# Attention stage of a two-layer diffusion step: adaLN weights in the ring, latent group first

## The reference, cut to what matters

```python
def ada_params(cvec, w, b):
    m = jax.nn.silu(cvec) @ w + b
    return jnp.split(m, N_ADA, axis=-1)

def modulate(x, g, shift, scale):
    return rms_norm(x, g) * (1.0 + scale[:, None, :]) + shift[:, None, :]

# layer 1, context tokens (group 0): 16 query heads on 4 key heads of 64, softmax with a sink logit
q, k, v = qkv_heads(h, wqkv, qn, kn)          # per-head RMS norm of q and k
s = einsum('bqkgd,bskd->bkgqs', qg, k) * HEAD_DIM ** -0.5
o = softmax([s, s_sink]) @ v;  y = o @ wo
# latent tokens (group 1): the same, q and k rotated (rope2d), keys = 128 own and 128 cached context keys
# then x = x + gate * y, and the MoE sub-layer with the last three of the six adaLN rows
```

## Time and profile before

| what | before |
|---|---|
| median of the runs | 1518.48 us (1517.93 to 1519.35) |
| the profiled execution, its own time | 1518.69 us |
| its span | 1516.9 us, so 1.8 us lie around it |
| mean granted TensorE clock | 0.948 of full |
| TensorE busy | 1429.9 us (94%) |
| VectorE, ScalarE busy | 461.3 us, 294.4 us |
| 16 DMA engines moved | 499.45 MB, 329 GB/s over the span |

### The profile page before, as it was taken

How to read it: one execution, slowest core, us unless ns; L and a number is a source line. 1 busy time by engine, 2 the same in 40 slices (tenths; PEclk the granted TensorE clock), 3 DMA queues, 4 the chain that set the end, 5 groups by cost and what they waited for, 6 DMA issues and landing times.

```text
span 1516.9 us, 23827 instructions
## 1 busy us (share of the span) xinstructions
PE 1429.9 (94%) x9544; PEld 851.1 (56%) x9544; DVE 461.3 (30%) x1449; ACT 294.4 (19%) x602; POOL 0.2 (0%) x4
## 2 busy tenths in 40 slices
PE   5798889999999999999888989999999999999997
PEld 2675775565555655556443647855565555555554
DVE  0699261222222222222234322522222222222222
ACT  2301241111111111111122212211111111111111
POOL 0000000000000000000000000000000000000000
PEclk8899889999999999999998569899999999999999
DMA  8989467699999999999744542796999999999990
GB/s 310 374 332 351 162 250 313 245 385 399 403 391 412 386 403 399 409 386 409 291 173 177 218 167 71 292 386 238 410 385 404 402 395 412 393 395 395 410 399 39
DMA packets 80640, 499.45 MB, mean 329 GB/s; under 512 B 10633, under 2 KB 15409, under 8 KB 23760
## 3 DMA queue, kind: packets, MB, share of 16 engines
q1 hardware_dynamic: 80592, 498.79, 82.2%
HBM read 497.45 MB, written 1.31 MB: 329 GB/s over the span
## 4 chain that ended last, share of the span: by engine, by line
PE 91%; DVE 5%; DMA 3%; ACT 1%; issue 1%; SPq 0%; DVEq 0%; ACTq 0%
PE ps L766 31%; PE ps L797 16%; PE ps L747 12%; PE ps L807 9%; PE ps L507 4%; PE ps L550 3%; PE ps L578 3%; PE ps L703 2%; PE ps L482 2%; PE ps L642 1%; PE ps L496 1%; PE ps L616 1%; DMA ring<-in_conv_w_dram 1%; DVE W L1188 1%; DVE hbf L1188 1%; PE ps L688 1%
## 5 line engine op out<-in xcount | busy, mean ns | idle before, releaser
L766 PE MATMUL ps<-ring,W 128*64 128x512 f32 x2048 | 453.3, 595 | 1.1 <-ACT W L1048 1.0
L766 PEld LDWEIGHTS ps<-ring,W 128*64 128x64 f32 x2048 | 166.2, 137 | 282.5 <-issue 277.6
L797 PE MATMUL ps<-ring,W 128*64 128x512 f32 x1024 | 233.9, 599 | 1.0 <-DVE W L1438 1.0
L747 PEld LDWEIGHTS ps<-W,hbf 128*128 128x128 bf16 x3168 | 183.1, 98 | 56.4 <-issue 54.2
L747 PE MATMUL ps<-W,hbf 128*128 128x128 bf16 x3168 | 199.2, 220 | 3.0 <-DVE W L1416 2.2
L1444 DVE TENSOR_TENSOR ypart<-ps,ypart 128x512 fp32r<-128x512 f32 x132 | 91.3, 692 | 191.0 <-ACT ypart L1059 191.0
L807 PE MATMUL ps<-comb,ypart 128*128 128x256 f32 x1056 | 142.5, 287 | 2.8 <-DVE ypart L1444 2.8
L1433 DVE SCALAR_TENSOR_TENSOR W<-W,ps 128x256 f32<-128x256 f32 x66 | 31.7, 480 | 352.1 <-ACT W L1053 352.1
L797 PEld LDWEIGHTS ps<-ring,W 128*64 128x64 f32 x1024 | 67.8, 136 | 117.5 <-issue 109.7
L807 PEld LDWEIGHTS ps<-comb,ypart 128*128 128x128 f32 x1056 | 130.2, 189 | 6.2 <-DVE ypart L1444 4.6
L1048 ACT ACTIVATE W<-ps 128x512 f32<-128x512 f32 x132 | 78.9, 597 | 273.7 <-PE ps L747 273.7
(11 more groups left out here) (196 smaller groups left out, 894.0 us busy)
## 6 DMA issues: line engine op xcount, KB each, us to landing
ring<-in_exp_w_gate_dram SPq DMA_DIRECT2D x128, 1024.0 KB, 8.8
ring<-in_exp_w_up_dram SPq DMA_DIRECT2D x128, 1024.0 KB, 10.8
ring<-in_exp_w_down_dram SPq DMA_DIRECT2D x128, 1024.0 KB, 9.7
S<-in_ada_w_dram SPq DMA_DIRECT2D x48, 1024.0 KB, 7.8
ring<-in_conv_w_dram SPq DMA_DIRECT2D x4, 2048.0 KB, 19.0
S<-in_attn_wqkv_dram SPq DMA_DIRECT2D x1, 6144.0 KB, 25.4
ring<-in_conv_w_dram SPq DMA_DIRECT2D x1, 4096.0 KB, 20.7
S<-in_exp_w_gate_dram SPq DMA_DIRECT2D x4, 1024.0 KB, 11.1
```

The lines of the kernel that those rows point to most:

```text
L747: mm = pe.matmul(PG[:, kk * P:(kk + 1) * P], hbf[:, part, g, 4 * half + kk, :], gbf[:, g, :], start=(n == 0), stop=(n == 2 * 3 - 1))
L766: mm = pe.matmul(PGU[64 * b:64 * b + 64, :].rearrange("p (h f) -> p h f", h=2), xg[:, k, 64 * b:64 * b + 64], gate_up_of(w[b])[:, k], star ...
L797: mm = pe.matmul(bank[64 * b:64 * b + 64, :], hidT[:, j, 64 * b:64 * b + 64], down_of(w[b])[:, j, n * 512:(n + 1) * 512], start=(j == 0), ...
```

## The change

The 16 late adaLN units no longer go to `S`. Units 32 to 37 go to ring slots 0 and 1 as soon as layer 0's pair 31 has done its down products (`pe_dn` 64), units 38 to 40 to ring slot 3 after the overflow pair's (`pe_dn` 66); units 41 to 47 reuse the same places as they are multiplied. TensorE multiplies units 32 to 35 ahead of the sum of squares, 36 to 39 behind it, 40 and 41 ahead of the head loop, and 42 to 47 in i = 0 to 5. Bank e = 4 is turned after the first three qkv products. Group 1 (latent) is multiplied, normed and transposed first, and the head loop runs its four heads first (`HEADS`). `wo` is loaded after the last qkv product. Experts 0 and 1 are loaded in the head loop (after units 43 and 46), experts 2 and 3 after the projection's first bank. `asq`, `prob`, `probT`, `oT`, `otok`, `stat` and the cached keys and values lie elsewhere, so that ring slot 3 is free.

```diff
@@ -67,7 +67,8 @@
 
     if u < EARLY:
         return u % 6
-    return u - EARLY if u < EARLY + 6 else 4 + u % 2
+    v = u - EARLY
+    return 6 + (v if v < 9 else v - 9)
 
 
...
+        ada_late = ring_f[:, 0:2 * EW].rearrange("p (s n) -> p s n", s=6)
+        ada_last = ring_f[:, 3 * EW:4 * EW].rearrange("p (s n) -> p s n", s=3)
+
+        def ada_unit(u):
+
+            slot = unit_slot(u)
+            if slot < 6:
+                return ada[:, slot, :]
+            return ada_late[:, slot - 6, :] if slot < 12 else ada_last[:, slot - 12, :]
 
         def diag(j):
...
@@ -215,21 +225,27 @@
         odd = hb_f[:, 2560:2816]
 
         arow = hT[:, 0:6, :].rearrange("p k t -> p (k t)").rearrange("p (b n) -> p b n", b=3)
+        arow_late = W[:, 3840:4352]
+
+        def ada_row(e):
+
+            return arow[:, e % 3, :] if e < 4 else arow_late
         xtok = ring_f[:, 16384:16384 + 2048].rearrange("p (g n) -> p g n", g=G)
         ytok = ring_f[:, 0:2048].rearrange("p (g n) -> p g n", g=G)
 
         B0 = 2 * EW
         qkv = ring_f[:, B0:B0 + 3072].rearrange("p (g n) -> p g n", g=G)
-        asq = ring_f[:, B0 + 3072:B0 + 5632].rearrange("p (g n) -> p g n", g=G)
-        prob = ring_f[:, B0 + 3072:B0 + 5120].rearrange("p (b h s) -> p b h s", b=2, h=QG)
-        otok = ring_f[:, B0 + 6912:B0 + 8960].rearrange("p (g n) -> p g n", g=G)
-        oT = ring_f[:, B0 + 8960:B0 + 11008].rearrange("p (k t) -> p k t", k=KC)
-        vctx = ring_f[:, B0 + 11008:B0 + 11264]
-        kctx = ring_f[:, B0 + 11264:B0 + 11520]
-        stat = ring_f[:, B0 + 11520:B0 + 11776]
+        otok = ring_f[:, B0 + 3072:B0 + 5120].rearrange("p (g n) -> p g n", g=G)
+        vctx = ring_f[:, B0 + 5120:B0 + 5376]
+        kctx = ring_f[:, B0 + 5376:B0 + 5632]
+        stat = ring_f[:, B0 + 5632:B0 + 5888]
+        asq = hb_f[:, 512:3072].rearrange("p (g n) -> p g n", g=G)
+        prob = hb_f[:, 512:2560].rearrange("p (b h s) -> p b h s", b=2, h=QG)
+        oT = hT
+        HEADS = [(1, j) for j in range(NKV)] + [(0, j) for j in range(NKV)]
         qTt = W[:, 0:2048].rearrange("p (c t) -> p c t", c=KC)
         kTt = W[:, 2048:2816].rearrange("p (c t) -> p c t", c=2)
-        probT = hb_f[:, 0:1024].rearrange("p (b n) -> p b n", b=2)
+        probT = W[:, 2816:3840].rearrange("p (b n) -> p b n", b=2)
 
         def half_of(part, h):
...
@@ -394,34 +410,40 @@
                     sp.wait_ge(moe_done, 1)
                     sp.dma_start(kctx, cache_k[0, 0].rearrange("t h d -> t (h d)")).then_inc(ld_kv, 16)
                     sp.dma_start(vctx, cache_v[0, 0].rearrange("t h d -> t (h d)")).then_inc(ld_kv, 16)
-                for s in range(2):
-                    load_expert(l, s, s, "gu")
-                for s in range(2):
-                    load_expert(l, s, s, "dn")
                 if l == 0:
+                    for s in range(2):
+                        load_expert(l, s, s, "gu")
+                    for s in range(2):
+                        load_expert(l, s, s, "dn")
                     sp.wait_ge(ada_used, EARLY)
                     load_shared(0)
                     sp.wait_ge(pj_out, 4)
+                    for s in range(2, 4):
+                        load_expert(l, s, s, "gu")
+                    for s in range(2, 4):
+                        load_expert(l, s, s, "dn")
                 else:
+                    load_ada(range(EARLY + 9, N_UNITS))
                     sp.wait_ge(at_qkv, 6)
-                    load_ada(range(EARLY, EARLY + 6))
-                    sp.wait_ge(at_nrm, 1)
-                    sp.wait_ge(at_copied, 1)
+                    sp.dma_start(wo, attn_wo[0].rearrange("(k p) n -> p k n", p=P)).then_inc(ld_wo, 16)
+                    sp.wait_ge(at_nrm, 2)
                     sp.dma_start(new_k[0, 0].rearrange("t h d -> t (h d)"),
                                  qkv[:, 0, NH * HD:(NH + NKV) * HD]).then_inc(stored, 16)
                     sp.dma_start(new_v[0, 0].rearrange("t h d -> t (h d)"),
                                  qkv[:, 0, (NH + NKV) * HD:QKVW]).then_inc(stored, 16)
-                    load_ada(range(EARLY + 6, EARLY + 8))
-                    sp.wait_ge(ada_used, EARLY + 4)
-                    sp.dma_start(wo, attn_wo[0].rearrange("(k p) n -> p k n", p=P)).then_inc(ld_wo, 16)
-                    load_ada(range(EARLY + 8, N_UNITS))
+                    for s in range(2):
+
+                        sp.wait_ge(ada_used, EARLY + 12 + 3 * s)
+                        load_expert(l, s, s, "gu")
+                        load_expert(l, s, s, "dn")
+                    sp.wait_ge(pj_out, 5)
+                    sp.wait_ge(ada_used, N_UNITS)
+                    sp.wait_ge(stored, 32)
+                    for s in range(2, 4):
+                        load_expert(l, s, s, "gu")
+                        load_expert(l, s, s, "dn")
                     sp.wait_ge(pj_out, 8)
                     load_shared(1)
-                    sp.wait_ge(stored, 32)
-                for s in range(2, 4):
-                    load_expert(l, s, s, "gu")
-                for s in range(2, 4):
-                    load_expert(l, s, s, "dn")
                 load_extra(l, 1)
...
+                    sp.wait_ge(moe_done, l + 1)
                 if l == 0:
-                    sp.wait_ge(pe_dn[0], 6)
+
                     sp.dma_start(wqkv, attn_wqkv[0].rearrange("(k p) n -> p k n", p=P)).then_inc(ld_qkv, 16)
+                    sp.wait_ge(pe_dn[0], 2 * PAIRS)
+                    load_ada(range(EARLY, EARLY + 6))
+                    sp.wait_ge(pe_dn[0], 2 * PAIRS + 2)
+                    load_ada(range(EARLY + 6, EARLY + 9))
             for g, y in enumerate((y_prompt, y_sample)):
                 sp.wait_ge(y_out, 2 * (g + 1))
...
@@ -533,7 +560,10 @@
 
             for l in range(L):
                 if l == 1:
+
+                    ada_products(range(EARLY, EARLY + 4), ps[2])
                     sum_squares(4, 0)
+                    ada_products(range(EARLY + 4, EARLY + 8), ps[2])
                 if l == 0:
 
...
@@ -589,26 +619,28 @@
                             mm.then_inc(at_tr, 1)
 
                     for n in range(3):
-                        qkv_product(0, n)
-                    qkv_product(1, 0)
-                    qkv_product(1, 1)
+                        qkv_product(1, n)
+                    ada_transposes(4, ps[2])
+                    qkv_product(0, 0)
+                    qkv_product(0, 1)
 
                     pe.wait_ge(ld_kv, 32)
                     for j in range(2):
                         mm = pe.transpose(ps[6][:, j * P:(j + 1) * P], kctx[:, j * P:(j + 1) * P], ident)
                     mm.then_inc(at_tr, 1)
-                    qk_transposes(0, ps[0:3])
-                    qkv_product(1, 2)
+                    pe.wait_ge(mod_ready, 5)
+                    qkv_product(0, 2)
+                    qk_transposes(1, ps[3:6])
 
                     def at_scores(i):
-                        g, j = divmod(i, NKV)
+                        g, j = HEADS[i]
                         keys = T if g == 0 else 2 * T
                         k0 = 0 if g == 0 else T
                         o = HD * (j % 2)
                         bk = 2 * (i % 2)
                         if i in (0, NKV):
                             pe.wait_ge(at_trc, 4 if i == 0 else 7)
-                        if i == 1:
+                        if i == 0:
                             pe.wait_ge(at_copied, 2)
                         if i >= 2:
                             pe.wait_ge(at_exp, i - 1)
...
                         mm.then_inc(at_s, 1)
 
                     def at_transposes(i):
-                        nk = 1 if i < NKV else 2
+                        nk = 1 + HEADS[i][0]
                         pe.wait_ge(at_exp, i + 1)
                         if i == 2:
...
@@ -645,26 +677,21 @@
                         mm.then_inc(at_o, 1)
 
 
-                    units = {i: range(36 + i, 37 + i) for i in range(4)}
-                    units |= {5: range(40, 43), 6: range(43, 46), 7: range(46, 48)}
                     pe.wait_ge(y_ready, KC)
                     at_scores(0)
                     at_scores(1)
-                    ada_products(range(EARLY, EARLY + 4), ps[7])
+                    ada_products(range(EARLY + 8, EARLY + 10), ps[7])
                     for i in range(G * NKV):
                         at_transposes(i)
                         if i + 2 < G * NKV:
                             at_scores(i + 2)
-                        if i == 4:
-                            ada_transposes(4, ps[7])
-                        if i == 5:
-                            pe.wait_ge(mod_ready, 5)
-                        ada_products(units.get(i, []), ps[7])
+                        if i < 6:
+                            ada_products([EARLY + 10 + i], ps[7])
...
@@ -973,13 +1000,13 @@
                         ins.then_inc(at_copied, 1)
 
                     def qk_roots(g):
```

(48 more changed lines are left out.)

8 lines of the change are left out of this document (3 added, 5 removed).

## The result

| | before | after |
|---|---|---|
| median of the runs | 1518.2 us (1517.45 to 1519.35) | 1504.73 us (1503.67 to 1505.89) |
| ratio of the times | | 0.9911, 95% interval 0.9894 to 0.9928 |
| the profiled execution, span | 1516.9 us | 1501.9 us |
| mean granted TensorE clock | 0.948 | 0.954 |

What follows compares the result with a forecast made beforehand. It took TensorE's work and clock as the bound, at half clock in layer 1's head loop. Start +2.1, qkv stage -2.6, gap -3.7, loop -44.9, tail +3.5: -45.6, giving 1473 us, range 1466 to 1502.

Steps and rivals of the forecast that it cites:

- Which level: Layer 1's head loop: clock falls once before it, units 40, 41 and transposes restore it; full clock throughout, 36.7 us.
- the rival at half clock: Head loop: clock falls in the idle time ahead and stays at half throughout; -18.4 us, or 1500; chance 28%.
- the forecast's course: Ahead of the head loop: clock falls first, then units 40 and 41 (3.7 us) and eight transposes bring it back.
- the forecast's kind: Outcomes with the loop's clock at full, or returning or falling part of the way; 1466 to 1488 us, 62%.
- Start of the qkv products: Layer 1: first qkv product expected at 770, 2.1 us later than the 767.85 of before.
- the bound by unit 39's landing: Qkv start: unit 39 lands at 770, which gives 770.9 as the latest start.
- qkv stage: Layer 1's qkv products: 41.8 us instead of 44.5, without the slow start and with changed transposes; end at 811.8.
- Gap ahead of the loop: From qkv products to head loop: 11.65 us instead of 15.35, as the norm ending last has no rotation.
- Loop at half clock: Head loop with units 32 to 41 and unit waits removed, all work at half clock: 64.8 us.
- Loop at full clock: Head loop with the same work at full clock: 35.7 us, 36.7 with 1 us for the start.
- Tail: Last transposes and projection's start at half clock after a fall in i = 6 and 7: +3.5 us; half-clock case 2.6.
- the bound of 0: Lower bound of the 3.5 us loss taken for the last transposes and the projection's start (bounds 0 and 5).

Runs made afterwards that it cites:

- Experiment 9: Changed kernel with one added wait: TensorE waits for the first head's exponentials before units 40 and 41, not behind them; 1480.67 us.
- Experiment 4: Changed kernel with each loop adaLN unit moved directly behind its head's transposes, ahead of the next scores; idle time not filled; 1479.22 us.
- experiment 1: Changed kernel plus five added matmuls of 512 columns, result unread, in TensorE's idle time ahead of the head loop; 1477.79 us.
- experiment 3: Changed kernel with the loads of units 32 to 40 issued only after the last matmul of layer 0's MoE; 1512.9 us.
- experiment 8: Experiment 7 with only units 32 and 33 loaded before layer 0's MoE ends, 36 to 39 multiplied behind the first three qkv products; 1472.71 us.
- experiment 7: Experiment 6 plus seven added matmuls of 512 columns, result unread, in the idle time ahead of the loop; 1473.59 us.
- experiment 6: Changed kernel with units 40 to 47 one in each loop head, directly behind its transposes, and none directly ahead of the loop; 1477.65 us.
- experiment 2: Changed kernel with units 42 to 47 also multiplied ahead of the head loop, so the loop holds no unit; 1488.03 us.

## Why the prediction was wrong

**The step that failed is "Which level".** It let the clock fall in the gap of 1.4 us behind the qkv products and in the scores, so that units 40 and 41 would be the run that brings it back. The gap was 1.17 us, the scores ran at 1.00, and so did the units. They were done 4.2 us before the exponentials, and the clock fell there, with transposes, scores, unit and values behind it, the order in which it did not rise from 828 to 888 in the kernel before. That is the rival at half clock, given 28% and 1500; the profiled execution took 1503.67, with 2.3 of the difference in the start of the qkv products and 1.1 in the loop. For a fall in so short a gap the prediction had no row. At 816.9 in the kernel before TensorE had stood idle from 814.1 on the earlier trace rows, about 2.8 us, and the prediction itself counts that row for the rival. A second fall in the kernel before, at 827.0, it passed over: 0.8 us into the idle time ahead of the loop, with 1.35 us idle ahead of the one unit before it. So "long idle time" was not the whole of what takes the clock either.

**The mechanism behind it held.** Experiment 9 makes the forecast's course come true by one wait, and the clock is back and stays until i = 6. Experiment 4 gets it back in the first head by order alone, experiment 1 never lets it go. These three end at 1477.8 to 1480.7, inside the 1466 to 1488 given for the forecast's kind. The prediction had named the loop's order as what keeps the clock down; experiment 4 shows it. Which property of the scores does that, their 64 rows or their length, no run tells apart.

**Start of the qkv products: 770 forecast, 772.32 measured,** in an execution that was 1.3 us ahead, so 3.6 us off. No unit was waited for; the bound by unit 39's landing never applied. The loss has two parts. The wait ahead of the last matmul of layer 0's MoE grew from 1.74 to 3.96 us (+2.2), which no step had. Experiments 3 and 8 show that it goes with the queue: 1.27 and 1.29 us where the units' loads do not stand in it at that moment, 3.91 to 4.16 in the changed kernel and the seven experiments where they do. In the window at 752 the DMA engines are busy all the time (share 1.02), in the same window before hardly at all (0.02). What is waited for is most likely a fetch of instructions that queues behind the weights. The traces list an instruction queue, and one packet of it (0.02 MB) passes 0.9 to 1.5 us after the start of layer 0's last combine in the three kernels where the queue is quiet, and 3.4 to 3.7 us after it in the other eight. In all eleven the next matmul starts 2.4 to 2.7 us behind that packet (in the changed kernel combine at 752.37, packet at 755.9, matmul at 758.50). Whose instructions they are the traces do not say, and no run moves that packet alone. The other part is the clock, lost in that wait: units 32 to 35 took 6.02 us, not 3.6. Together the two parts are 4.6 us; the forecast had 1.4 us in hand for a late unit, which was not needed.

**qkv stage: right** (42.10 for 41.8). The products began at full speed, with units and squares ahead of them.

**Gap ahead of the loop: right** in length (11.23 for 11.65). But the first two heads' scores took 2.94 us, not 3.8, so more of it was idle, which counted against the clock.

**Loop at half clock: right** (65.96 for 64.8). No unit was waited for; what is left is waits for VectorE's copies in i = 6 and 7 (0.78 to 1.46 us).

**Loop at full clock: a little low.** 35.7 was worked out and 38.2 measured in experiment 7, which has a unit in i = 6 and 7 too (with the end, these two heads are 1.6 of the 2.5).

**Tail: right for the case** (+2.7 for 2.6). Behind the forecast's own loop, at full clock up to i = 6, it was +2.0 in experiment 1, where 3.5 was taken. The full loop's tail in experiment 6 was as the bound of 0 said, once a unit stood in the last heads.

**The Trainium skill (TensorE: Matmul & The Clock Gate, Part 4) does not agree with these traces where it says that the full clock does not engage for transposes:** eight transposes take 1.04 us in experiment 1 and 1.97 in the changed kernel, so the 5 us that the prediction set against it are not paid. They also help to bring the clock back: in experiment 4 it rises 1.3 us into the unit behind eight transposes, in experiment 9, without transposes ahead, only 3.2 us into the units.

## What to carry to other kernels

Where a stage runs at half clock, look for the idle time that takes the clock and for the order that keeps it down before taking out work or waits: here the whole change gave 13.5 us, and one more wait, or another order of the same calls, gave 24 to 27 more. Work that can stand anywhere (the adaLN units here) is best spent one piece in each head, behind the transposes, and in the idle stretches that would cost the clock, or right behind them as in experiment 9, not ahead of them. When loads are moved earlier, look at what else goes through the DMA engines at that moment.

## What the hardware did that was not expected

- A wait of TensorE that no semaphore explains, at the change from layer 0's MoE to layer 1, took 1.27 to 1.74 us with a quiet queue and 3.91 to 4.16 us with weights queued. A packet of the instruction queue always lay 2.4 to 2.7 us ahead of the matmul that ended it.
- The clock stayed at 1.00 through the gap of 1.17 us and the narrow scores behind it in every kernel with the latent group first, and fell in the idle times of 4.2 us and more ahead of the loop. Yet in experiment 2, without units in the loop, it was lost behind a wait of 0.64 us, and in the kernel before at 827.0, 0.8 us into an idle time.
- In the idle time ahead of the loop the clock fell after 4.0 us in the changed kernel and experiment 4, where units 40 and 41 stand ahead of it, and after 2.4 to 2.5 us in experiments 9 and 6, where scores do. That the units are the reason is not shown.
- In experiment 4 the clock came back from 0.50 within one unit behind eight transposes. In the changed kernel the same two kinds of work, with scores between them, did not raise it in 65 us, although TensorE was busy for 61.54 of them.
